# FFN turns: the first part of the end sums made by GpSimd in SBUF, all four banks evicted by ScalarE

## Time and profile before

| what | value |
|---|---|
| median of 3 runs | 2352.56 us (2352.56 to 2352.81) |
| the profiled execution | 2351.54 us, its span 2349.7 us |
| TensorE busy | 2342.6 us |
| VectorE busy | 1911.8 us |
| ScalarE busy | 1521.1 us |
| GpSimd busy | 43.7 us |

### The profile page before, as it was taken

The page is one execution under the profiler, slowest core; times in us unless marked ns, Lnnn a source line. Parts: engine busy times, 40 slices in busy tenths (PEclk is TensorE's granted clock), DMA queues, the critical chain, the costliest instruction groups (busy, mean ns, idle before and its releaser), DMA issues.

```text
span 2349.7 us, 28124 instructions
## 1 busy us (share of the span) xinstructions
PE 2342.6 (100%) x10566; PEld 1943.7 (83%) x10566; DVE 1911.8 (81%) x2325; ACT 1521.1 (65%) x1821; POOL 43.7 (2%) x49
## 2 busy tenths in 40 slices
PE   9999999999999999999999999999999999999999
PEld 8888888888888888888888888888888888888887
DVE  6898889798887766767666778888989988897878
ACT  6666666764567765666676566576666666754665
POOL 0000000000000000000021000010000000000010
PEclk9999999999999999999999999999999999999999
DMA  7776767766577654877786777686676778666775
GB/s 249 208 231 201 219 206 217 225 201 213 183 229 200 200 167 140 222 223 206 217 202 162 215 214 208 196 242 205 197 232 203 216 218 230 200 206 196 225 211 179
DMA packets 319364, 488.54 MB, mean 208 GB/s; under 512 B 138424, under 2 KB 140416, under 8 KB 319232
## 3 DMA queue, kind: packets, MB, share of 16 engines
q1 hardware_dynamic: 318784, 486.47, 69.7%
q10 hardware_dynamic: 448, 0.34, 0.1%
HBM read 453.70 MB, written 2.10 MB: 194 GB/s over the span
## 4 chain that ended last, share of the span: by engine, by line
PE 98%; DVE 1%; ACT 0%; issue 0%; DMA 0%; POOL 0%; POOLq 0%; ACTq 0%
PE ps L696 38%; PE ps L718 12%; PE ps L720 12%; PE ps L719 12%; PE ps L845 7%; PE ps L847 7%; PE ps L846 7%; PE ps L1104 1%; PE ps L1092 1%; PE ps L914 0%; DVE wl L1853 0%; ACT wh L1244 0%; PE ps L1225 0%; DMA raw<-in_w_o 0%; DVE res L2048 0%
## 5 line engine op out<-in xcount | busy, mean ns | idle before, releaser
L1853 DVE TENSOR_TENSOR wl<-raw,wh 128x1024 fp32r<-128x1024 f32 x764 | 925.2, 1225 | 352.3 <-ACT wh L1244 347.4
L1244 ACT ACTIVATE wh<-raw 128x1024 fp32r<-128x1024 f32 x763 | 796.6, 1054 | 511.6 <-PE ps L696 226.8
L718 PE MATMUL ps<-wh,hT 128*128 128x512 f32 x1156 | 451.7, 391 | 0.8 <-DVE vd L2155 0.5
L720 PE MATMUL ps<-wh,hT 128*128 128x512 f32 x1156 | 450.0, 389 | 0.0
L719 PE MATMUL ps<-wl,hT 128*128 128x512 f32 x1156 | 449.9, 389 | 0.0
L696 PE MATMUL ps<-wh,hT 128*128 128x512 f32 (+1 forms) x1456 | 392.3, 387 | 0.3 <-DVE vd L2155 0.3
L696 PEld LDWEIGHTS ps<-wh,hT 128*128 128x128 f32 x1456 | 269.1, 188 | 53.7 <-DVE vd L2155 0.5
L718 PEld LDWEIGHTS ps<-wh,hT 128*128 128x128 f32 x1156 | 217.1, 188 | 46.1 <-DVE vd L2155 0.9
L720 PEld LDWEIGHTS ps<-wh,hT 128*128 128x128 f32 x1156 | 217.0, 188 | 45.3
L719 PEld LDWEIGHTS ps<-wl,hT 128*128 128x128 f32 x1156 | 217.1, 188 | 44.7
L696 PE MATMUL ps<-wl,hT 128*128 128x512 f32 x728 | 222.0, 386 | 0.0
(11 more groups left out here) (449 smaller groups left out, 3376.1 us busy)
## 6 DMA issues: line engine op xcount, KB each, us to landing
raw<-in_w_in SPq DMA_DIRECT2D x208, 512.0 KB, 4.1
raw<-in_w_up SPq DMA_DIRECT2D x176, 512.0 KB, 4.6
raw<-in_w_down SPq DMA_DIRECT2D x176, 512.0 KB, 4.5
raw<-in_w_gate SPq DMA_DIRECT2D x175, 512.0 KB, 4.0
raw<-in_w_o SPq DMA_DIRECT2D x32, 512.0 KB, 4.7
raw<-in_w_ple_gate SPq DMA_DIRECT2D x32, 512.0 KB, 4.4
raw<-in_w_br_mla SPq DMA_DIRECT2D x16, 512.0 KB, 4.1
raw<-in_w_br_dil SPq DMA_DIRECT2D x16, 512.0 KB, 5.0
```

Source lines behind the costliest of these rows:

```text
L718: pe.matmul(ps[:, b0 + t, :], xh, wh[:, s, c], start=first, stop=False)
L720: mm = pe.matmul(ps[:, b0 + t, :], xl, wh[:, s, c], start=False, stop=last)
L1244: act.activation(wh[:, j % SLOTS, :], raw[:, j % SLOTS, :], ACT.Copy).then_inc(hi_ready, 1)
L1853: dve.tensor_tensor(wl[:, j % SLOTS, :], raw[:, j % SLOTS, :], wh[:, j % SLOTS, :].bitcast(F32), ALU.subtract).then_inc(lo_ready, 1)
```

## The change

For each of the 18 fast turns (nine in each FFN), after unit 11:

- ScalarE copies all four banks b1 to b1+3 into `ends`, in three instructions (512, 512 and 1024 columns), and signals `p1_out` after the second and `g1_free` after the third. From the second fast turn on it first waits for the product of the turn before (`am_ready`), which reads `ends`.
- `first_ends` of VectorE is gone. GpSimd makes the same combinations from SBUF with four adds of 128 x 512, each waiting for the one before it through `ends_step`; the last signals `ends_sum`. A new tile `both_end` (2 KB) holds the intermediate sum.
- `turn_ends` on VectorE waits for `ends_sum` in place of `g1_free`.
- GpSimd's queue: the nine turns of the first FFN stand ahead of all its copies, those of the second between `right(2)` and `right(3)`.

```
+            def ends_of(n):
+                pool.wait_ge(p1_out, n + 1)
+                pool.tensor_tensor(both_end[:, :], ends[:, 0, :], ends[:, 3, :], ALU.add).then_inc(ends_step, 1)
+                pool.wait_ge(ends_step, 3 * n + 1)
+                pool.wait_ge(g1_free, n + 1)
+                pool.tensor_tensor(ends[:, 1, :], ends[:, 1, :], both_end[:, :], ALU.add).then_inc(ends_step, 1)
+                pool.wait_ge(ends_step, 3 * n + 2)
+                pool.tensor_tensor(ends[:, 3, :], ends[:, 2, :], ends[:, 1, :], ALU.add).then_inc(ends_step, 1)
+                pool.wait_ge(ends_step, 3 * n + 3)
+                pool.tensor_tensor(ends[:, 2, :], ends[:, 2, :], both_end[:, :], ALU.add).then_inc(ends_sum, 1)
+
+            for n in range(len(FAST_TURNS)):
+                ends_of(n)
             right(1)
...
             right(2)
+            for n in range(len(FAST_TURNS), 2 * len(FAST_TURNS)):
+                ends_of(n)
             right(3)
...
                         if v == 2 * FAST_PAIRS[-1] + 1:
                             act.wait_ge(fast_done, fasts(f, m + 1))
-                            act.activation(ends[:, 0, :], ps[:, free_bank(m + 1), :], ACT.Copy).then_inc(p1_out, 1)
+                            done = f * len(FAST_TURNS) + m - 1
+                            if done:
+                                act.wait_ge(am_ready, T * (f * FFN_TURNS + m))
+                            b1 = free_bank(m + 1)
+                            act.activation(ends[:, 0, :], ps[:, b1, :], ACT.Copy)
+                            act.activation(ends[:, 3, :], ps[:, b1 + 1, :], ACT.Copy).then_inc(p1_out, 1)
+                            act.activation(ends[:, 1:3, :], ps[:, b1 + 2:b1 + 4, :], ACT.Copy).then_inc(g1_free, 1)
...
-                    if m in FAST_TURNS and v == 2 * FAST_PAIRS[-1] + 1:
-                        first_ends(f, m)
...
-            def first_ends(f, m):
-
-                b1 = free_bank(m + 1)
-                dve.wait_ge(p1_out, f * len(FAST_TURNS) + m)
-                chain(dve.tensor_tensor(ends[:, 3, :], ps[:, b1 + 1, :], ends[:, 0, :], ALU.add))
-                both = ends[:, 3, :].unsqueeze(1).to_broadcast([P, 2, BANK])
-                chain(dve.tensor_tensor(ends[:, 1:3, :], ps[:, b1 + 2:b1 + 4, :], both, ALU.add))
-                dve.tensor_tensor(ends[:, 3, :], ps[:, b1 + 3, :], ends[:, 1, :], ALU.add).then_inc(g1_free, 1)
-
             def turn_ends(units, m, ends_before):
                 dve.wait_ge(unit_done, units)
-                dve.wait_ge(g1_free, ends_before + m)
+                dve.wait_ge(ends_sum, ends_before + m)
```

More of the change, by code:

```diff
@@ L156, in hybrid_layer @@
         TH, TL = at("TH", 28 * KB, [P, 4, BANK], F32R), at("TL", 36 * KB, [P, 4, BANK], F32R)
+        both_end = at("both_end", 98 * KB, [P, BANK])
         whole_x, forms = at("whole_x", 28 * KB, [P, 3, 2, S]), at("forms", 36 * KB, [P, 4, 3, P])
@@ L261, in hybrid_layer @@
             sem(n) for n in ("sig_ready", "am_ready", "a_raw", "ah_ready", "a_ready"))
-        forms_raw, forms_hi, forms_ready, sums_ready, TH_ready, TL_ready, fast_done, p1_out, g1_free, ends_ready, ups_out, a_forms_raw, a_forms_hi, a_forms_ready, g1_out = (
+        forms_raw, forms_hi, forms_ready, sums_ready, TH_ready, TL_ready, fast_done, p1_out, g1_free, ends_ready, ups_out, a_forms_raw, a_forms_hi, a_forms_ready, g1_out, ends_sum, ends_step = (
             sem(n) for n in ("forms_raw", "forms_hi", "forms_ready", "sums_ready", "TH_ready", "TL_ready", "fast_done",
-                             "p1_out", "g1_free", "ends_ready", "ups_out", "a_forms_raw", "a_forms_hi", "a_forms_ready", "g1_out"))
+                             "p1_out", "g1_free", "ends_ready", "ups_out", "a_forms_raw", "a_forms_hi", "a_forms_ready", "g1_out", "ends_sum", "ends_step"))
         planes_ready, planes_in = sem("planes_ready"), sem("planes_in")
```

## The result

The changed kernel takes 2358.56 us (median of 13 runs, 2355.37 to 2360.43), the kernel before, run beside it, 2351.96 (13 runs, 2350.68 to 2353.56). The ratio is 1.0027, 95% interval 1.0020 to 1.0034, or 4.7 to 8.0 us: 6.6 us slower. That is over the 0.2% (4.7 us) that the forecast took as the bound of a change, with the interval's lower end on it. The forecast was +1.6, 2354.2 us and "same", with a range of 2351.5 to 2360.

The account below looks back on a forecast made before the run. TensorE, busy for all but 7 us, was taken as the bound. Three turns' lateness, 0.24 + 0.94 + 0.29 = 1.5 us, and a tenth for GpSimd's own waits gave +1.6: 2352.56 + 1.6 = 2354.2 us, range 2351.5 to 2360.

Parts of the forecast that it names:

- same: Outcome with the time within 0.2%, 4.7 us, of the kernel before; chance 0.70, of which 0.4 for a visible cost.
- the 16 stops: TensorE's weight loads waiting before the first fast pair of a turn, 4.4 us in all; removable loss likely 0.5 to 2 us.
- A small cost, as forecast: ScalarE's two added evictions, taken as 1.46 us a turn, delay its roundings: cost 0 in turn 1, 0.67 us in turn 6.
- GpSimd holds VectorE: GpSimd instructions and VectorE subtractions with both inputs in SBUF don't overlap; late turns cost 1.5 us, with GpSimd's own wait 1.6.
- the needed lead: Time needed from first eviction's start to unit 2's split on VectorE: 7.69 us at 1.2 us an add; less makes it late.
- three and 1.5: Late turns 1, 6 and 7 of the first FFN: 0.24 + 0.94 + 0.29 = 1.5 us.
- leads a us shorter by other landings: Sign of failure: times from first eviction to unit 2's split come out a us shorter because landings have moved.
- the slower one: Rival: GpSimd's adds get into every turn; about +12 us, 2365, at 1.5 us an add; chance 0.26.
- its first form: Four adds and the splits between don't fit ahead of unit 2's split; from about 1.35 us an add, 4.8 us in all.
- the likeliest case's own range: 2352.5 to 2357.4 us, from the two bounds of a GpSimd add, 0.61 and 1.35 us.
- Its second form: VectorE's ready instruction goes first, so `turn_ends` waits for `ends_sum`, up to 1.2 us a turn; five turns +6, sixteen +19.
- Faster: Rival: VectorE, freed of 2.6 us a turn, releases `turn_ends` earlier; 2350.5 us even if all stops vanished; chance 0.04.

Follow-up runs that it names:

- no_adds: The changed kernel with GpSimd's four adds left out, `turn_ends` waiting for `g1_free`, output not the reference's; 2353.22 us, ratio 1.0008.
- vector_adds: The changed kernel with the same four adds from SBUF made by VectorE at the place of `first_ends`, GpSimd idle; 2352.51 us, ratio 1.0002.
- before_adds_2: The kernel before with four unused GpSimd adds a turn, each reading two different tiles, `turn_ends` waiting for them; 2360.41 us, ratio 1.0036.

## Why the prediction was right in its mechanism and short in its size

- **Where the time could go.** Right: TensorE's work is unchanged, and the rise of the profiled run (5.1 of 5.3 us) is in the 16 stops that the prediction named, by way of the split of unit 2, the sums and `turn_ends`.
- **ScalarE.** A small cost, as forecast: 0.67 us, all in turn 6; no_adds has 1.5 us by the medians with an interval from -0.5 to 4.0, vector_adds 0.1 (-1.6 to 2.6). The two further evictions hold ScalarE 1.35 us (90.01 - 88.15 less the 0.51 of one) where 1.46 was taken.
- **GpSimd holds VectorE.** Shown: the adds, not the evictions, make nearly all of the rise (no_adds, vector_adds, before_adds_2), each add after the second and each split waiting the other out.
- **The term that was mis-sized: the step from an add's time to the needed lead.** The add was put at 1.2 us, between 1.04 and 1.35; it is 1.29, and by the prediction's own sum (0.6 us of lead for 0.15 us an add) that alone is 0.36 us of lead. A held split ends 1.08 us after the add, not 1.02, and a held add 1.15 after the split, where 1.2 - 0.13 = 1.07 was taken. Three splits, three held adds and one free add make 3 x 0.06 + 3 x 0.08 + 0.09, 0.5 us: the lead from first eviction to unit 2's split that is needed is 14.39 less the 6.18 from that split to the fast pair (101.39 - 95.21) = 8.21 us, not 7.69. With the leads of the kernel before that makes seven late turns and 4.2 us in place of three and 1.5. The threshold turns half a us into a factor of three, since the leads are crowded just above it.
- **The rest, about 2 us.** The leads were taken from one execution, and the prediction itself named leads a us shorter by other landings as a sign of failing. In the profiled run after, the late turns are others in part: turn 5 of the second FFN had 14.51 us from first eviction to fast pair before, and without its wait of 1.23 it would have 13.16 after; turn 6 of the first, forecast as the worst, waits only 0.24. The evictions stand behind splits that wait for loads, and when these land differs: in turn 1, before any add, the eviction starts at 88.15 and not 87.76. Whether the held splits also delay loads of later turns was not followed. That the runs of the changed kernel spread over 5.1 us and those of before over 2.9 fits.
- **The rivals.** By the bound of 4.7 us the slower one (0.26) came true in place of "same" (0.70), in its first form: the adds and splits don't fit ahead of unit 2's split. It was to decide from about 1.35 us an add, for 4.8 us; it did so at 1.29, where the corrected sum has 4.2. That it sets in gradually from below, and that the leads scatter, was priced too low. The measured 2358.56 us lies inside the range of 2351.5 to 2360 only because that range reached into the slower rival; the likeliest case's own range ended at 2357.4. Its second form, VectorE going first when both wait, didn't occur. "Faster" stayed out: nothing was gained from the 47 us of work that VectorE lost.
- **The page's figure.** The Trainium skill, "GPSIMD Engine Reference", section "3.1 Elementwise — side-by-side cycle accounting": the estimate of 1.12 us, scaled from its 4497 ns for 2048 elements, is under the 1.29 measured here. With a fixed part of 0.19 us, as the copies have the earlier trace rows, taken off before scaling and added again, the estimate would have been 0.19 + 1.08 = 1.27. Its advice to leave elementwise work to VectorE is borne out: VectorE does one of these adds in 0.69 us, and vector_adds has +0.1 us.

## What to carry to other kernels

Work given to an idle engine isn't free if its instructions and the busy engine's can't overlap: count each one's length into the busy engine's row, and look whether a point with no slack (here a stop of TensorE at the same place in every turn) lies behind it. Where the margin differs from turn to turn, price by the distribution of the margins, from more than one execution, and not by the one mean: near the threshold a small error in a duration is a large one in the time. Work moved off a bound row should be short, and the place to look for is where the engine that stays reads PSUM, or stands idle; that such a place would make the four adds free is argued from the rows and wasn't shown.

## What the runs showed of the hardware

- A GpSimd f32 add of 128x512 took 1.29 us with two different inputs and 1.04 with the same tile twice. Whether that is a saved read wasn't tried further.
- When a VectorE instruction with both inputs in SBUF and a GpSimd add wait for each other again and again, they alternate (ends 1.15 and 1.08 us apart by turns): neither was passed over in any of the turns read, though VectorE's next split was ready.
- A VectorE add with one input in PSUM ran at its usual 0.68 to 1.23 us during GpSimd's adds, where splits, 1.22 us when free, took up to 2.33.
